# A decoder layer's mixer takes its groups of key tiles two at a time: both turns, then values, then both scores, then both shares of the projection

## The reference, cut to what matters

```python
for i in range(S // Q_BLOCK):                       # 16 blocks of 128 queries
    z = jnp.einsum('bhqd,bhkd->bhqk', qb, kb) * scale   # keys up to the block's end
    mask = s_idx < t_idx
    log1m = jnp.where(mask, jax.nn.log_sigmoid(-z), 0.0)
    between = lax.cumsum(log1m, axis=3, reverse=True) - log1m
    attn = jnp.where(mask, jnp.exp(jax.nn.log_sigmoid(z) + between), 0.0)
    outs.append(jnp.einsum('bhqk,bhkd->bhqd', attn.astype(vb.dtype), vb))
```

## Time and profile before

| | us |
|---|---|
| median of 3 runs | 2816.57 (2816.51 to 2819.57) |
| profiled execution: time | 2813.91 |
| profiled execution: span, first to last instruction | 2812.3 |
| PE busy over the span | 2507.2 (89%) |
| DVE, ACT, POOL busy over the span | 1479.4, 1114.9, 816.4 |
| PE waiting for POOL at a turn (line 752), whole span | 19.2, in 19 waits |
| PE waiting for DVE at a turn (line 752), whole span | 6.4, in 10 waits |

### The profile page before, as it was taken

One profiled execution on the slowest core, in us unless ns is written; L12 is line 12 of the kernel. 1 busy time (PEld: TensorE's weight loads), 2 busy tenths in 40 slices (PEclk: granted clock), 3 DMA queues, 4 the chain that ended last, 5 costly groups with the idle time before them and its releaser, 6 DMA issues. The chain is left out here.

```text
span 2812.3 us, 36346 instructions
## 1 busy us (share of the span) xinstructions
PE 2507.2 (89%) x12521; PEld 2092.3 (74%) x12522; DVE 1479.4 (53%) x1898; ACT 1114.9 (40%) x1814; POOL 816.4 (29%) x703
## 2 busy tenths in 40 slices
PE   5999789999999999999968969983998999999970
PEld 4788578878888888888857758773887888888750
DVE  6122156666566656566632256765446544526636
ACT  2122244545454545454520012112456545536633
POOL 2111022442222222222301235456222222223236
PEclk9999899999999999999989989995999999999985
DMA  7699966766757574746456646423467655636735
GB/s 265 243 317 311 308 201 193 245 207 214 220 174 216 177 232 159 214 152 199 146 185 221 175 152 230 144 98 120 136 185 237 206 145 175 208 89 208 255 75 239
DMA packets 259931, 553.75 MB, mean 197 GB/s; under 512 B 23989, under 2 KB 93737, under 8 KB 259177
## 3 DMA queue, kind: packets, MB, share of 16 engines
q1 hardware_dynamic: 236904, 486.74, 52.4%
q0 software_dynamic: 15248, 46.62, 7.6%
q10 hardware_dynamic: 7664, 18.88, 1.7%
HBM read 399.14 MB, written 153.02 MB: 196 GB/s over the span
## 5 line engine op out<-in xcount | busy, mean ns | idle before, releaser
L92 PE MATMUL mx_acc<-u_u,mx_w_hi 128*128 128x512 f32 x1792 | 569.5, 399 | 0.9 <-DMA mx_w_lo<-halves 0.6
L700 POOL TENSOR_TENSOR mx_wt<-mx_wt,mx_rest 128x127 f32<-128x127 f32 (+15 forms) x128 | 271.5, 2121 | 764.7 <-DVE mx_rest L907 764.7
L92 PEld LDWEIGHTS mx_acc<-u_u,mx_w_hi 128*128 128x128 f32 x1792 | 325.0, 189 | 65.5 <-DMA mx_w_lo<-halves 1.9
L915 DVE TENSOR_TENSOR mx_wt_lo<-mx_p_t,mx_wt_hi 128x512 fp32r<-128x512 f32 (+2 forms) x320 | 192.3, 605 | 317.4 <-ACT mx_wt_hi L870 315.6
L92 PE MATMUL mx_acc<-u_u,mx_w_lo 128*128 128x512 f32 x896 | 351.7, 393 | 0.0
L870 ACT ACTIVATE mx_wt_hi<-mx_p_t 128x512 fp32r<-128x512 f32 (+2 forms) x320 | 171.0, 534 | 415.8 <-PE mx_p_t L752 358.5
L907 DVE TENSOR_TENSOR_SCAN mx_rest<-mx_rest,mx_zero 128x128 f32<-128x128 f32 (+15 forms) x128 | 312.1, 2438 | 11.4 <-ACT mx_wt L852 11.4
L92 PE MATMUL moe_p_gu<-moe_gu_hi,moe_x_hi 128*128 128x512 f32 x656 | 262.3, 400 | 15.1 <-DVE moe_gu_lo L1883 13.0
L92 PE MATMUL moe_p_gu<-moe_gu_hi,moe_x_lo 128*128 128x512 f32 x656 | 258.2, 394 | 0.0
L92 PE MATMUL moe_p_gu<-moe_gu_lo,moe_x_hi 128*128 128x512 f32 x656 | 258.0, 393 | 0.0
L851 ACT ACTIVATE mx_rest<-mx_p_z 128x512 f32<-128x512 f32 (+2 forms) x320 | 171.0, 534 | 96.3 <-PE mx_p_z L739 59.3
(11 more groups left out here) (244 smaller groups left out, 5160.6 us busy)
## 6 DMA issues: line engine op xcount, KB each, us to landing
mx_w_hi<-halves SPq DMA_DIRECT2D x102, 512.0 KB, 3.9
mx_w_lo<-halves SPq DMA_DIRECT2D x102, 512.0 KB, 5.2
keep_stay<-in_w_gate SPq DMA_DIRECT2D x64, 512.0 KB, 4.3
keep_stay<-in_w_up SPq DMA_DIRECT2D x64, 512.0 KB, 5.2
keep_stay<-in_w_down SPq DMA_DIRECT2D x32, 1024.0 KB, 6.8
halves<-fr_ring SPq DMA_DIRECT2D x36, 512.0 KB, 6.5
u_saved<-u_u SPq DMA_DIRECT2D x4, 4096.0 KB, 19.5
mx_w_mod<-in_w_ada SPq DMA_DIRECT2D x64, 256.0 KB, 5.1
```

The lines of the kernel that those rows point to most:

```text
L92: mm = pe.matmul(out, a, b, start=first and n == 0, stop=last and n == len(pairs) - 1, skip_group_check=True)
L700: pool.tensor_tensor(wt[:, t % 2, 0:w - 1], wt[:, t % 2, 0:w - 1], rest[:, t % 2, 1:w], ALU.mult).then_inc(m["weights_done"], 1)
L915: dve.tensor_tensor(wt_lo[:, first:first + k - j], p_t[:, n % TR, 0:(k - j) * P].rearrange("p (j t) -> p j t", t=P), f32(wt_hi[:, first:fi ...
```

## The change

A table `CHUNKS_OF[t]` cuts the groups of tile t into twos; with one or three groups, the last chunk has one. PE, ACT and DVE then take a chunk where they took a group. POOL's and SP's lists stay as they are. The amount of work is the same; only the order on three engines differs.

```diff
--- before.py
+++ after.py
@@ -430,6 +430,7 @@
 PAIR_GROUPS = [GROUPS[2 * g + 1] for g in range(PG)]
 PG_BEFORE = [sum(PAIR_GROUPS[:g]) for g in range(PG + 1)]
 NV = PG_BEFORE[PG]
+CHUNKS_OF = [[range(a, min(a + 2, GROUPS[t])) for a in range(0, GROUPS[t], 2)] for t in range(NT)]
 CYCLE = ("cx", "cc", "gate", "cb", "gate", "gate", "gate")
 UNITS_HEAD = 2 * len(CYCLE)
 FILL_BASE, FILL_STEP = 3.0, 0.5
@@ -811,16 +812,22 @@
                 scores(0, t, range(GROUPS[t]))
             for h in range(HEADS):
                 for t in range(NT):
-                    for r in range(GROUPS[t]):
-                        turn(h, t, r)
-                        if t % 2 == 1 and r > 0:
-                            values(h, t // 2, r - 1)
-                        if t % 2 == 0 and r == 0 and t > 0:
-                            values(h, t // 2 - 1, PAIR_GROUPS[t // 2 - 1] - 1)
-                        ha, ta = ahead_of(h, t)
-                        scores(ha, ta, ahead_banks(h, t, r))
-                        fill(h, GR_BEFORE[t] + r)
-                values(h, PG - 1, PAIR_GROUPS[PG - 1] - 1)
+                    ha, ta = ahead_of(h, t)
+                    for chunk in CHUNKS_OF[t]:
+                        for r in chunk:
+                            turn(h, t, r)
+                        if t % 2 == 1 and chunk[0] > 0:
+                            for r in range(chunk[0] - 2, chunk[0]):
+                                values(h, t // 2, r)
+                        if t % 2 == 0 and chunk[0] == 0 and t > 0:
+                            for r in CHUNKS_OF[t - 1][-1]:
+                                values(h, t // 2 - 1, r)
+                        for r in chunk:
+                            scores(ha, ta, ahead_banks(h, t, r))
+                        for r in chunk:
+                            fill(h, GR_BEFORE[t] + r)
+                for r in CHUNKS_OF[NT - 1][-1]:
+                    values(h, PG - 1, r)
                 sum_mod(h)
             pe.wait_ge(m["mod_step"], 2)
 
@@ -886,13 +893,16 @@
                 sigmoids(0, t, range(GROUPS[t]))
             for h in range(HEADS):
                 for t in range(NT):
-                    for r in range(GROUPS[t]):
-                        high(h, t, r)
-                        ha, ta = ahead_of(h, t)
-                        sigmoids(ha, ta, ahead_banks(h, t, r))
-                        for n in ended(h, GR_BEFORE[t] + r):
-                            out_unit(n)
-                            high_w(n + 2)
+                    ha, ta = ahead_of(h, t)
+                    for chunk in CHUNKS_OF[t]:
+                        for r in chunk:
+                            high(h, t, r)
+                        for r in chunk:
+                            sigmoids(ha, ta, ahead_banks(h, t, r))
+                        for r in chunk:
+                            for n in ended(h, GR_BEFORE[t] + r):
+                                out_unit(n)
+                                high_w(n + 2)
 
         @block.vector
         def _(dve):
@@ -971,17 +981,19 @@
             scan(0, 0)
             for h in range(HEADS):
                 for t in range(NT):
-                    for r in range(GROUPS[t]):
-                        low(h, t, r)
-                        if r == 0:
+                    for chunk in CHUNKS_OF[t]:
+                        for r in chunk:
+                            low(h, t, r)
+                        if chunk[0] == 0:
                             if t + 1 < NT:
                                 scan(h, t + 1)
                             elif h + 1 < HEADS:
                                 scan(h + 1, 0)
                             if t % 2 == 0 and t > 0:
                                 output(h, t // 2 - 1)
-                        for n in ended(h, GR_BEFORE[t] + r):
-                            out_unit(n)
+                        for r in chunk:
+                            for n in ended(h, GR_BEFORE[t] + r):
+                                out_unit(n)
                     if t % 2 == 0:
                         add_mod(h * KD + t // 2)
                 output(h, PG - 1)
```

## The result

The changed kernel takes 2835.38 us (median of 4 runs, 2834.07 to 2837.24) where the kernel before takes 2817.32 (4 runs, 2816.51 to 2819.57): 1.0064 times, with a 95% interval of 1.0052 to 1.0077. It is slower by 18 us. The profiled execution took 2835.07 us, span 2833.5.

What follows compares the result with a forecast made beforehand. The prediction took the mixer to be bound by PE, each tile lasting as long as PE's list or the scan-weigh chain. Eight heads of +2.48 us (19.8), less 1.4, gave +18.4 on 2816.6: 2835.0 us, range 2822 to 2851 (8 in 10).

Steps and rivals of the forecast that it cites:

- The terms of a head: Changes in length of tiles 4 to 8 and 12 to 14 in each mixer head, summing to +2.48 us.
- The chain of low, scan, weigh and turn: DVE to POOL to PE: a second low of 512 columns delays the scan, and so the next turn, by 0.61 us.
- Values into the tile behind: Values groups moved on PE from tiles 5, 7, 13 into 6, 8, 14: +0.95, +0.95 and, in tile 13, -0.95 us.
- The margins in tiles 6 and 8: PE's list outlasts the delayed chain by 0.1 us or less; rival that this fails: 2840 to 2855, chance 0.12.
- Pairing at nothing: Pairing turns on PE saves nothing; at most 0.02 us for each of 128 pairs, 2.6 us in all.
- The second head's -1.4: Second head, tile 13, PE-bound: the wait of values for DVE's low part goes, saving 1.4 us once.
- The clock: PE's clock in the mixer: no term; rival of falls costing 5 us in each of 7 or 8 heads, 2870, chance 0.03.
- The total: Whole kernel: 2.48 us a head, 19.8 in eight heads, less 1.4: +18.4 us, to 2835.0.
- What it would show: Signs in the changed profile: scans 8 and 15 at 2.5 us after the turn, POOL waits some 35 us, head 134.4 us.
- A granted clock under 1.00 inside the mixer: Sign that would show the prediction wrong, as it expected the clock to stay at 1.00 in the mixer.

Runs made afterwards that it cites:

- scan_back_mid: Changed kernel with the scan, and the output that follows it, behind the first low again in tiles 0 to 11; 2824.00 us, 1.0031.
- values_moved_alone: Kernel before, unpaired, with only the values of group 0 of pairs 2 and 3 moved from tiles 5 and 7 into 6 and 8; 2826.91 us, 1.0039.
- values_back: Changed kernel with the values of group 0 of pairs 2 and 3 back in tiles 5 and 7; 2823.84 us, 1.0029.
- both_back: Changed kernel with the scan behind the first low in tiles 4 to 11 and group 0's values of pairs 2 and 3 back in tiles 5 and 7; 2816.95 us, 1.0007.
- scan_back_all: Changed kernel with the scan behind the first low in every tile, those of four groups too; 2863.93 us, 1.0169.
- single_scan_first: Kernel before, unpaired, with the scan ahead of the low in even tiles and tiles 1, 3, 5, convolution output behind the second low; 2821.07 us, 1.0027.
- scan_first_late_conv: Changed kernel with the scan ahead of both lows in all tiles, and the convolution's output behind scan and lows in tiles 4 and 12; 2804.54 us, 0.9967.
- pairs_best: Changed kernel, scan first everywhere, convolution output behind the scan in tile 4, behind both lows in 12, tile 12's output behind the fourth low; 2803.32 us, 0.9957.
- scan_first: Changed kernel with the scan ahead of both lows, except in tile 12; 2813.19 us, 0.9991.
- output_first: Changed kernel with the output of the pair before ahead of the scan on DVE in even tiles; 2896.52 us, 1.0286.
- single_best: Kernel before, scan first in even tiles, 1, 3; convolution output behind scan in tile 4, first low in 12; tile 12's output behind third low; 2807.14 us, 0.9973.

## Why the prediction was right, step by step

The forecast was 2835.0 us, the measured median 2835.38. The terms of a head, forecast and measured in us (changed kernel less before, from the table): tile 4 +0.20 and +0.20; tile 5 +0.04 and +0.03; tile 6 +0.95 and +1.02; tile 7 +0.16 and +0.15; tile 8 +0.95 and +0.97; tile 12 +0.52 and +0.50; tile 13 -0.95 and -1.06; tile 14 +0.61 and +0.60. The sum was to be 2.48; the whole head, as the sum of the medians, grew by 2.44.

- **The chain of low, scan, weigh and turn** was right, with its 0.05 us at the end. scan_back_mid takes the delay out of tiles 4, 5 and 7, and it goes as the sum had it.
- **Values into the tile behind**: right in kind, shown by values_moved_alone and by tile 8 of values_back. The size was slightly low: a group is worth 0.97 to 1.06, where 0.95 was taken.
- **The margins in tiles 6 and 8** held. Turn 7 starts 0.21 us after its weigh; turn 9, at 957.50, doesn't wait either.
- **Pairing at nothing** was right: both_back stands at 1.0007 with all the pairs in place.
- **The second head's -1.4** is the one term that did not show in the profiled execution. The wait of values for low did go, and yet tile 13 of that head shortened by 0.98 us, not by 0.95 + 1.4. DVE in the tile before, then PE at the turn:

```profile
580.28 3.56 DVE L959 SCALAR_TENSOR_TENSOR mx_conv<-mx_gated,keep_conv_cols,mx_conv 128x512 f32<-128x512 f32 x2
583.76 1.28 DVE L925 TENSOR_TENSOR mx_wt_lo<-mx_p_t,mx_wt_hi 128x512 fp32r<-128x512 f32 x2
584.96 3.88 DVE L917 TENSOR_TENSOR_SCAN mx_rest<-mx_rest,mx_zero 128x1792 f32<-128x1792 f32 x1
```
```profile
592.33 1.60 PE L753 MATMUL mx_p_t<-keep_ident,mx_wt 128*128 128x128 f32 x8 [2.51 <-POOL mx_wt L701]
```

  The convolution's two operations take 3.56 us there, for 1.54 in the fifth head, so the lows and scan 13 behind them are late. (POOL makes a weight's low part beside them, from 579.83 to 582.51, and is idle at this place of the fifth head; that this is the cause was not tried.) Before, PE spent this time in two pieces, 2.10 us at turn 3 of tile 12 and 1.4 at the values of tile 13. Now it spends 2.51 in one piece at turn 13. From 592.80 on, 3.40 us run at a granted clock of 0.50 (the first row of windows above), which costs half of them, 1.7 us. Tile 13 is 13.91 us there for 12.31 elsewhere: 1.6. In both_back the same turn waits the same 2.51 us, and no fall follows; the turn, and the window of the whole tile 13:

```profile
588.75 1.09 PE L753 MATMUL mx_p_t<-keep_ident,mx_wt 128*128 128x128 f32 x8 [2.51 <-POOL mx_wt L701]
```
```profile
588.75:601.10 12.35, 12.35 (x70) 10.69 (x71) 7.76 (x7) 7.10 (x13) 7.05 (x3) 1.00 0.03 11
```

  There the tile takes 12.31 us for the 14.89 of before, 2.6 less where 0.95 + 1.4 was the forecast; scan_back_mid has 12.31 too. So the term itself holds, and in the changed kernel's profiled execution it was given back to the clock, which the prediction had at nothing.
- **The clock** was a rival at 0.03 and did not decide, but it came twice in a small way. The second time is in the third head: PE waits 1.06 us for `mx_w_lo` to land at 633.21, and from 633.70 on 3.40 us run at 0.50 (1.7 us lost). Tile 0 of that head takes 5.38 us for 3.12. The DMA engines were busy 0.80 of the 33 us before it and 0.96 of these 3.4, where the fifth head has 0.65.
- **The total** came nearer than its parts. The second and the third head together grew by 8.4 us where 2 * 2.48 - 1.4 = 3.6 was forecast; the other six by 12.5 where 14.9 was, the heads one by one by 1.6 to 2.5. So the first error is +4.8 and the second -2.4, which makes up for half of it. The sum for the profiled executions was 18.4, and their spans differ by 21.2. The medians differ by 18.1. That this comes within 0.3 us of the sum is luck: against the spans the sum is 2.8 us short, and the executions of one kernel lie 3 us apart in the first measurement and up to 15 us in the later ones (before: 2808.52 to 2823.23).
- **What it would show**: nearly all seen. Scan 8 starts 2.47 us after the turn (2.5 forecast), the high of tile 6 at 2.04 and of tile 8 at 2.15 us into the tile (2.1), a turn's wait for POOL adds up to 38.2 (35), for DVE to 0.4; the fifth head lasts 134.0 (134.4). "A granted clock under 1.00 inside the mixer" was named as a sign against the prediction; it appeared in two stretches of 3.4 us, and the one in the second head is what hid the term of -1.4.

## What to carry to other kernels

Where an engine takes its list in order, changing the grouping of a loop changes what stands ahead of the one operation that the next stage waits for. Find that operation (here the scan), look at its start against the start of the stage, and keep it ahead of everything that is only wanted later: moving it ahead of the lows and of the convolution turned a loss of 0.6% into a gain of 0.4%, with the same grouping, and the like moves without the grouping gained 0.3%. Work moved between stages pays only if the stage that loses it is bound by that engine; out of a stage that another chain sets, into one that this engine sets, it is a loss of its full length, less what slack the first stage gives back (1.06 and 1.02 us paid, 0.30 and 0.45 given back in values_moved_alone).

## What the hardware showed that I had not expected

- A wait of PE was followed by a stretch at the lower clock in one head or kernel, and the same wait was not in another. The 2.51 us in the second head were followed by 3.4 us at 0.50 in the changed kernel, and by no fall in both_back and scan_back_mid. In scan_back_all seven heads have a wait of 3.07 or 3.08 us, and in five of them the clock fell, in some before the wait was over. In single_scan_first six heads have a wait of 1.94 us, and five a fall behind it. Where the same tile can be compared with and without one, a stretch of 3.4 us cost 1.6 us (13.91 for 12.31, 9.88 for 8.31). The 38 shorter waits for POOL in the changed kernel, of 0.43 to 1.48 us, were followed by no fall, but one of 1.06 us for a landing was; before the change one of 2.10 us was not. So the length of one wait does not decide alone, and what else does was not tried. The Trainium skill (TensorE: Matmul & The Clock Gate, section "A second HAM failure mode: psum-queue depth-cycling") has the clock swing with frequent short idles; in these rows the frequent idles near 1 us did not do that, and falls came mostly in or behind single waits of 1.9 us and more.
- Waits for `mx_w_lo` were longer in every paired kernel that was faster than the changed one (2.6 us in both_back, 4.0 in scan_back_mid, 4.3 in values_back, 5.6 in scan_first_late_conv, 5.8 in pairs_best, 7.1 in scan_first, for 2.0 in the changed kernel), and output_first, the slowest, had 0.3. They took back part of each gain. Speed alone does not order them: single_best, nearly as fast as pairs_best, had 2.4, and the kernel before 0.6. Whether the transfers' start or their bandwidth is at fault stays open.
